# State space heads: difference and minimum as one two-step operation per chunk, C's exponential and product first, the late convolution behind the products

## The reference, cut to what matters

```python
a_cum = cumsum(dt * A)                        # per chunk and head
seg = a_cum[l] - a_cum[s]                     # token l, earlier token s
decay = exp(where(causal, seg, -inf))
y_diag = einsum((C . B) * decay, X)           # inside a chunk
y_off = einsum(C, state before the chunk) * exp(a_cum)
y = y_diag + y_off + D * xs
```

## Time and profile before

| | us |
|---|---|
| median of 3 runs | 3256.41 |
| lowest, highest | 3252.58, 3259.01 |
| the profiled execution | 3257.33 |
| its span, from the first to the last instruction | 3255.5 |
| TensorE busy | 3144.8 |
| VectorE busy | 1563.5 |
| ScalarE busy | 911.5 |
| GpSimd busy | 1211.7 |

### The profile page before, as it was taken

One profiled execution on the slowest core, in us unless ns is written; L12 is line 12 of the kernel. 1 busy time (PEld: TensorE's weight loads), 2 busy tenths in 40 slices (PEclk: granted clock), 3 DMA queues, 4 the chain that ended last, 5 costly groups with the idle time before them and its releaser, 6 DMA issues.

```text
span 3255.5 us, 39350 instructions
## 1 busy us (share of the span) xinstructions
PE 3144.8 (97%) x15256; PEld 2582.3 (79%) x15256; DVE 1563.5 (48%) x2373; ACT 911.5 (28%) x1481; POOL 1211.7 (37%) x940
## 2 busy tenths in 40 slices
PE   8999999998999899899999999999999999999999
PEld 5778888887787677688888888788788878878887
DVE  5765666566435786642221333325314455454343
ACT  4454444444212232400223323201101232210000
POOL 3332122211366422233232232354335668753332
PEclk9999999999999999999999999999999999999999
DMA  3321011010144221154222232421113433342222
GB/s 138 98 81 40 27 31 35 27 33 26 63 130 145 79 72 57 48 165 158 68 61 69 62 82 59 130 72 52 46 46 123 156 120 115 116 188 97 104 97 84
DMA packets 110774, 276.21 MB, mean 85 GB/s; under 512 B 9088, under 2 KB 35328, under 8 KB 109200
## 3 DMA queue, kind: packets, MB, share of 16 engines
q1 hardware_dynamic: 60768, 207.64, 20.1%
q10 hardware_dynamic: 49840, 66.21, 6.3%
HBM read 233.81 MB, written 40.01 MB: 84 GB/s over the span
## 4 chain that ended last, share of the span: by engine, by line
PE 88%; DVE 8%; ACT 2%; issue 1%; DMA 1%; ACTq 0%; SPq 0%; DVEq 0%
PE proj_bank L233 17%; PE proj_bank L235 17%; PE proj_bank L234 17%; PE proj_bank L3137 4%; PE proj_bank L3138 4%; PE proj_bank L3139 4%; PE aux_banks L233 3%; PE aux_banks L234 3%; PE aux_banks L235 3%; PE aux_banks L3123 2%; PE aux_banks L3125 2%; PE aux_banks L3124 2%; PE aux_banks L783 2%; PE aux_banks L864 2%; PE aux_banks L790 1%
## 5 line engine op out<-in xcount | busy, mean ns | idle before, releaser
L233 PE MATMUL proj_bank<-h_hi,slab_hi 128*128 128x512 f32 x2400 | 954.6, 398 | 17.2 <-DVE ffn_made L3016 7.1
L235 PE MATMUL proj_bank<-h_hi,slab_lo 128*128 128x512 f32 x2400 | 937.0, 390 | 0.0
L234 PE MATMUL proj_bank<-h_lo,slab_hi 128*128 128x512 f32 x2400 | 936.4, 390 | 0.0
L255 POOL CAST slab_hi<-slab_raw 128x1024 fp32r<-128x1024 f32 x234 | 251.7, 1076 | 1713.6 <-PE proj_bank L235 1196.3
L259 POOL TENSOR_TENSOR slab_lo<-slab_raw,slab_hi 128x512 fp32r<-128x512 f32 x468 | 651.4, 1412 | 18.8
L233 PEld LDWEIGHTS proj_bank<-h_hi,slab_hi 128*128 128x128 f32 x2400 | 451.9, 188 | 128.5 <-issue 19.1
L235 PEld LDWEIGHTS proj_bank<-h_hi,slab_lo 128*128 128x128 f32 x2400 | 451.5, 188 | 96.6
L234 PEld LDWEIGHTS proj_bank<-h_lo,slab_hi 128*128 128x128 f32 x2400 | 452.4, 188 | 91.7 <-issue 2.2
L3137 PE MATMUL proj_bank<-ffn_hi,ff_hi 128*128 128x512 f32 x512 | 199.4, 389 | 3.2 <-DVE ffn_lo L3199 3.2
L3139 PE MATMUL proj_bank<-ffn_hi,ff_lo 128*128 128x512 f32 x512 | 199.2, 389 | 0.0
L3138 PE MATMUL proj_bank<-ffn_lo,ff_hi 128*128 128x512 f32 x512 | 199.2, 389 | 0.0
(11 more groups left out here) (447 smaller groups left out, 5064.3 us busy)
## 6 DMA issues: line engine op xcount, KB each, us to landing
slab_raw<-wts SPq DMA_DIRECT2D x236, 512.0 KB, 3.6
ffn_made<-ffn_made ACTq DMA_DIRECT2D x64, 256.0 KB, 2.5
ff_raw<-wts SPq DMA_DIRECT2D x32, 512.0 KB, 3.8
ffn_raw<-ffn_made SPq DMA_DIRECT2D x8, 2048.0 KB, 8.8
ada_w<-ada_w SPq DMA_DIRECT2D x40, 384.0 KB, 3.2
ada_w_early<-ada_w SPq DMA_DIRECT2D x24, 384.0 KB, 3.6
ssd_decay_rows<-decay_sums ACTq DMA_DIRECT2D x16, 512.0 KB, 3.8
dil_rows<-dilated_out ACTq DMA_DIRECT2D x12, 520.0 KB, 8.2
```

The source lines that it names most:

```text
L233: pe.matmul(bank, whi[:, slot, wk, :], hi[:, xk, cols], start=first and a == 0, stop=False)
L234: pe.matmul(bank, whi[:, slot, wk, :], lo[:, xk, cols], start=False, stop=False)
L235: mm = pe.matmul(bank, wlo[:, slot, wk, :], hi[:, xk, cols], start=False, stop=last and a == len(ks) - 1)
L255: pool.tensor_copy(whi[:, to], k.raw[:, slot]).then_inc(k.s_hi, 1)
```

## The change

Three edits, all in `ssd_mix_stage`. In `weigh` the two operations of 1024 columns become eight of 128 columns, each subtracting the column of its own chunk (a scalar for each partition) and taking the minimum with zero in a second step; the wait between the two goes. In `weights_exp` and `mask` C's exponential and C's product come before those of the weights; as ScalarE no longer comes behind `weigh` with C's exponential, it waits itself for the row, for the pair before, and at a group's start for the reads of what it writes over. In the first group `conv(4 + n)` moves from between `weigh(n)` and `mask(n)` to behind `mask(n)`.

```diff
         def weights_exp(g, n):
             for h in range(g * GH + 2 * n, g * GH + 2 * n + 2):
+                act.wait_ge(s_ab[h % 2], 16 * (h // 2 + 1))
+                if h // 2:
+                    act.wait_ge(s_y, h // 2)
+                if h == g * GH:
+                    act.wait_ge(s_bc, (g + 1) * CHUNKS)
+                if h == g * GH + 1:
+                    act.wait_ge(s_st, (g + 1) * CARRIED)
+                act.activation(c_decayed(g, h % 2), ab[:, h % 2], ACT.Exp).then_inc(s_exp, 1)
                 act.wait_ge(s_seg, h + 1)
                 act.activation(m[:, h % 2], m[:, h % 2], ACT.Exp).then_inc(s_exp, 1)
-                act.activation(c_decayed(g, h % 2), ab[:, h % 2], ACT.Exp).then_inc(s_exp, 1)
...
-                    col = k.acol[:, :, h:h + 1].broadcast_to([P, CHUNKS, P])
-                    mc = m[:, h % 2].rearrange("p (c l) -> p c l", c=CHUNKS)
-                    v.settle(dve, dve.tensor_tensor(mc, ab[:, h % 2].rearrange("p (c l) -> p c l", c=CHUNKS), col, ALU.subtract))
-                    dve.tensor_scalar(m[:, h % 2], m[:, h % 2], 0.0, None, ALU.min).then_inc(s_seg, 1)
+                    for c in range(CHUNKS):
+                        cols = slice(c * P, (c + 1) * P)
+                        ins = dve.tensor_scalar(m[:, h % 2, cols], ab[:, h % 2, cols], k.acol[:, c, h:h + 1], 0.0, ALU.subtract, ALU.min)
+                    ins.then_inc(s_seg, 1)
...
                     dve.wait_ge(s_exp, 2 * h + 1)
-                    dve.tensor_tensor(m[:, h % 2], m[:, h % 2], cb.rearrange("p c l -> p (c l)"), ALU.mult).then_inc(s_m, 1)
-                    dve.wait_ge(s_exp, 2 * h + 2)
                     own = c_decayed(g, h % 2)
                     dve.tensor_tensor(own, own, k.cv[:, g, :], ALU.mult).then_inc(s_m, 1)
+                    dve.wait_ge(s_exp, 2 * h + 2)
+                    dve.tensor_tensor(m[:, h % 2], m[:, h % 2], cb.rearrange("p c l -> p (c l)"), ALU.mult).then_inc(s_m, 1)
...
                 weigh(n)
+                mask(n)
                 if g == 0:
                     conv(4 + n)
-                mask(n)
                 if n:
                     out(n - 1)
```

## The result

The changed kernel takes 3239.58 us (median of five runs, 3238.84 to 3243.83) against 3256.41 for the kernel before (3252.58 to 3261.36, on the same chip): ratio 0.9946, interval 0.9935 to 0.9956, 17 us less.

The account below looks back on a forecast made before the run. TensorE, busy 97% of the span, was taken as the bound, with about 20 us of waits for VectorE and lost clock within reach; the terms summed to -11.0 us, from 3256.41 to 3245.4 us, range for 8 in 10 3240 to 3255.

Parts of the forecast that it names:

- short operation, start to start: VectorE's weighing: 0.20 us for each operation of 128 columns, a pair in 3.2 us against 3.73.
- pair 0, first group, wait: TensorE's 5.03 us wait for VectorE's mask falls to about 0.4 us behind the projections: -4.6 us.
- its clock: First group, pair 0: the products' clock drop behind the 5.03 us wait goes: -1.2 us.
- pairs 1 to 3, waits: First group: with the convolution behind the mask, a chain of 8.0 us under 11.2 of projections; waits go, -2.1 us.
- new wait for the evacuation: Behind first-group pair 0: late convolution and SiLU delay ScalarE's evacuation of the bank the next piece needs, +0.6 us.
- pair 2, wait: Second group: the short operations cut the wait by 0.5 us, to 2.4.
- pair 3, wait: Second group: -0.5 by short operations, -1.4 by only one mask product held by GpSimd's cast; the wait becomes 2.8 us.
- clock of pairs 2 and 3: Second group: of 4.06 us lost to the lower clock behind the waits, 1.5 saved, bounds 0 and 4.1.
- the two answers that cost nothing: C's exponential and product first: no gain, no cost; later first-group evacuations done 12.1 us after a pair, wanted at 14.8.
- more: Rival, chance 0.14: short operations at 0.14 us, clock never falling in the second group; -16.2 us, 3240.2.
- slower: Rival, chance 0.09: every short instruction takes 0.386 us, 6.2 us a pair; +5.5 us, 3261.9.
- The estimate of 0.13 us an operation: By the Trainium skill's formula, 58 cycles and half the columns at 0.96 GHz: a pair 2.0 us, more gain than forecast.

Follow-up runs that it names:

- the short operations alone: Kernel before with only the eight short operations in place of the difference and the minimum, convolution and order unchanged: 3248.86 us, ratio 0.9972.
- the version with the moved pieces: Changed kernel with projection pieces 24 and 25 ahead of second-group pair 2, 26 and half of 27 ahead of pair 3: 3238.06 us, ratio 0.9937.

## Why the prediction was wrong, though most of its mechanism held

The steps on VectorE's chain and on the waits held; the gain was a half larger than forecast, 16.8 us for 11.0. The measured 3239.58 us lies 0.4 us below the range for 8 in 10, 3240 to 3255; timed again on another chip the changed kernel took 3242.22. Step by step, from the profiles of before and after (us):

| step of the prediction | forecast | measured |
|---|---|---|
| short operation, start to start | 0.20 | 0.20 |
| pair 0, first group, wait | -4.6 | -5.0 |
| its clock | -1.2 | -1.35 |
| pairs 1 to 3, waits | -2.1 | -2.1 |
| new wait for the evacuation | +0.6 | +0.3 |
| second group, pair 0 | +0.2 | 0.0 |
| pair 2, wait | -0.5 | -0.65 |
| pair 3, wait | -1.9 | -2.5 |
| clock of pairs 2 and 3 | -1.5 | -4.4 |
| sum | -11.0 | -15.8 |

**The step that failed** is the clock of the second group: "With two waits of 2.4 and 2.8 I take 1.5 saved, bounds 0 and 4.1." The products of both pairs ran at 1.00 in all three profiles of the changed kernel, so that the whole loss of before was saved: 4.4 us, and 2.9 of the 4.8 us by which the sum is off. The step took a value between two outcomes, one seen at pair 2 and the other at 2902 to 2908. The runs show in its place that waits between 2.2 and 3.8 us go either way, and that behind a wait of 2.3 us a fall cost 1.67 us (1.53 once) or nothing. None, one or two falls in the changed kernel would have saved 4.4, 2.8 or 1.1 us; the 1.5 stands near two falls, which the short operations alone showed behind the same waits in two of three profiles. What decides between these outcomes stays open. From the one profile of before this could not be read: its loss at pairs 2 and 3 was 4.4 us, in the two later profiles of the same kernel 2.4 and 4.2.

The loss was also read too small. The stretch from which the prediction takes 3.61 us for a pair at 1.00 ends at 1200.65, but the next projection of the kernel before starts earlier:

```profile
1200.46 0.50 PE L233 MATMUL proj_bank<-h_hi,slab_hi 128*128 128x512 f32 x1
```

From the head at 1197.04 a pair at 1.00 takes 3.42 us. The losses of before are then 1.35, 1.67 and 2.77 us, 5.8 and not 5.2; the table counts them so.

Smaller errors lie in GpSimd's share. *Pair 0*: the short operations were expected to be held until about 1171.1; they ended at 1170.7, and the mask at 1175.2 instead of 1175.75, ahead of the projections' end (each in its own profile; this one's stage starts 0.3 us later than that of before). With that the convolution and the evacuation came earlier as well, 0.26 of wait and not 0.6. GpSimd's two splits gained with them. Its timeline in the changed kernel, the split at pair 0 and the cast at pair 3, against the earlier trace rows:

```profile
1165.37 2.54 POOL L259 TENSOR_TENSOR slab_lo<-slab_raw,slab_hi 128x512 fp32r<-128x512 f32 x2
...
1322.90 2.93 POOL L255 CAST slab_hi<-slab_raw 128x1024 fp32r<-128x1024 f32 x1 [16.96 <-PE proj_bank L235]
```

The splits took 3.52 us beside the long operations. *Pair 3*: the forecast left one mask product held by the cast; none was. VectorE's last two masks of pair 3 in the changed kernel, beside this cast, against 2.06 and 2.28 in the earlier trace rows:

```profile
1322.59 1.21 DVE L2002 TENSOR_TENSOR ssd_c_decayed<-ssd_c_decayed,ssd_conv_out 128x1024 f32<-128x1024 f32 x1
1323.72 1.21 DVE L2004 TENSOR_TENSOR ssd_weights<-ssd_weights,ssd_cb 128x1024 f32<-128x1024 f32 x1
```

Here the cast was held (2.93 us, 1.22 before) and VectorE was not. So the wait fell to 2.26, by 2.47 us and not 1.9.

From the last product that waits for VectorE's states in the first group (1156.30) to the first projection behind the last pair (1344.28) the stage took 188.0 us before, and 171.8 after (1156.62 to 1328.42): 16.2 saved, 0.4 beyond the table, spread over the pairs in pieces of about 0.1. The other 1.6 of the 17.8 us lie outside the stage, at waits that are no part of the change (those for VectorE's `ffn_made` fell from 7.1 to 5.5 us). A second profile of the changed kernel, whose stage took 171.8 us again, took 3244.36 us. In it TensorE was busy for 3144.5 us with the same instructions, 5.0 more than in the first, and behind the stage its granted clock was 0.99 for 1.00: the clock elsewhere in the kernel also moves single executions by some us.

Right were also the two answers that cost nothing: the order is worth nothing (ratio 0.9999), though with less room than was worked out, and no projection behind pairs 1 to 3 waits for ScalarE. The room: behind pair 0 the fourth exponential ended at 1185.78, 6.5 us after the pair and not 5.2, just ahead of the mask that reads it (1186.01); the two evacuations and a table load of 1.28 us came first. Of the rivals, "more" had the size (3240.2) and the clock, but not its 0.14 us an operation, and it took 1.3 us too much off the waits of pairs 2 and 3, so that the fit of its total is in part luck; "slower" fell with the 0.20. The estimate of 0.13 us an operation, which stands beside the forecast, was not met either.

## What to carry to other kernels

Where a stage alternates between two engines, sum the chain of the slower one between two hand-overs and set it against the cover; then first move out of the chain what nobody waits for soon, as the convolution here (-13 us by the ratio for a move of two lines), and only then make what is left faster. A clock that fell behind a short wait is not a price to be charged by the microsecond: look at several profiles of the same kernel, and keep both outcomes in the range. What doesn't hang on it is to give the wait a cover: in the one profile of the version with the moved pieces both late pairs started without a wait for VectorE and ran at 1.00.

## What was not expected of the hardware

- Behind the same wait the granted clock differs: 2.96 us in three profiles of one kernel gave 0.63, 1.00 and 0.50 in the 3.6 us behind it; 3.76 us was followed by 1.00 and 2.31 us by 0.56. Ten of ten waits of 4.7 us or more were followed by a lower clock.
- Beside GpSimd's splits sixteen short operations of VectorE took 5.0 us for 3.2 alone, and the splits 2.54 us where they had taken 3.52 beside the long ones. Which of two engines is held turned between the kernels: before, VectorE's last two masks of pair 3 lost 1.9 us beside a cast that had started 0.24 us ahead of them (1333.53, 1333.77) and the split behind it; in the changed kernel, where a mask started 0.31 us ahead (1322.59, 1322.90), the cast lost 1.7 and the masks nothing. With the short operations alone both lost at pair 0, where a mask started 0.02 us ahead: the cast took 2.10 us and the mask behind it 2.06. That the order of the starts decides it was not tried.
